# A second feed-forward in two phases: up products partly as seven block products, down products by token

## What is computed

```python
def conv_ffn(h, w_up, conv_w, conv_b, w_down):     # h: 1024 x 1024, w_up: 1024 x 5632, w_down: 2816 x 1024
    u = h @ w_up
    up = jnp.pad(u, ((0, 0), (CONV_W // 2, CONV_W // 2), (0, 0)))
    u = sum(up[:, j:j + T] * conv_w[j] for j in range(CONV_W)) + conv_b      # CONV_W = 3
    gate, val = jnp.split(u, 2, axis=-1)
    return (jax.nn.silu(gate) * val) @ w_down

    f = conv_ffn(modulate(x, mod[3], mod[4]), w_up[l], conv_w[l], conv_b[l], w_down[l])
    x = layer_norm(DEEPNORM_ALPHA * x + mod[5] * f, ln2_g[l], ln2_b[l])
```

## Time and profile before

| | |
|---|---|
| runs (3), median | 3620.06 us (3619.49 to 3621.11) |
| profiled execution, span | 3623.1 us, 3.0 above that median |
| TensorE busy | 3438.2 us, 95% of the span |
| VectorE, ScalarE, GpSimd busy | 47%, 29%, 30% |
| DMA | 186.44 MB, 51 GB/s in the mean |

### The profile page before, as it was taken

How to read it: one execution, slowest core, us unless ns; L and a number is a source line. 1 busy time by engine, 2 the same in 40 slices (tenths; PEclk the granted TensorE clock), 3 DMA queues, 4 the chain that set the end, 5 groups by cost and what they waited for, 6 DMA issues and landing times.

```text
span 3623.1 us, 57600 instructions
## 1 busy us (share of the span) xinstructions
PE 3438.2 (95%) x24727; PEld 2833.2 (78%) x24727; DVE 1690.8 (47%) x2711; ACT 1040.3 (29%) x1485; POOL 1077.2 (30%) x412
## 2 busy tenths in 40 slices
PE   6999999988999999999999899999979989999998
PEld 5777778877778888888887677788867678888887
DVE  4333563066276343343436732463086764434436
ACT  4333564124232111111113323474143321111111
POOL 1221101302343333333333212201313344444443
PEclk9999999989999999999999899999989999999999
DMA  5111001252211111111111111001152111111111
GB/s 192 33 23 30 1 2 59 88 188 59 60 30 41 35 39 38 35 41 36 36 41 70 23 26 39 11 2 30 47 177 79 50 47 47 47 47 51 49 47 64
DMA packets 269680, 186.44 MB, mean 51 GB/s; under 512 B 45404, under 2 KB 249076, under 8 KB 269428
## 3 DMA queue, kind: packets, MB, share of 16 engines
q1 hardware_dynamic: 268272, 182.28, 16.8%
q10 hardware_dynamic: 1156, 0.48, 0.0%
HBM read 174.33 MB, written 8.39 MB: 50 GB/s over the span
## 4 chain that ended last, share of the span: by engine, by line
PE 84%; DVE 9%; issue 3%; ACT 1%; DMA 1%; POOL 1%; SPq 1%; POOLq 0%; DVEq 0%; ACTq 0%
PE psum L1146 61%; PE psum L937 6%; PE psum L1252 5%; PE psum L1410 3%; PE psum L946 2%; PE psum L1338 2%; DVE f_t L2490 1%; PE psum L1174 1%; DMA ada_late<-in_w_ada_dram 1%; DVE y_chan L2376 1%; PE psum L1369 1%; PE psum L1072 1%; DVE c_x L2340 1%; DVE h_lo L2116 1%; PE psum L1494 1%
## 5 line engine op out<-in xcount | busy, mean ns | idle before, releaser
L1146 PE MATMUL psum<-h_hi,w_split 128*128 128x512 f32 (+1 forms) x6016 | 1458.4, 370 | 15.8 <-DVEq L696 6.2
L887 POOL TENSOR_SCALAR w_split<-w_raw 128x1024 fp32r<-128x1024 f32 x196 | 550.3, 2808 | 2371.2 <-PE psum L1146 1640.8
L1146 PEld LDWEIGHTS psum<-h_hi,w_split 128*128 128x128 f32 x6016 | 1038.3, 188 | 229.4 <-issue 20.6
L1146 PE MATMUL psum<-h_lo,w_split 128*128 128x512 f32 (+1 forms) x3008 | 806.8, 368 | 0.0
L1146 PEld LDWEIGHTS psum<-h_lo,w_split 128*128 128x128 f32 x3008 | 520.0, 188 | 98.0
L2490 DVE SCALAR_TENSOR_TENSOR f_t<-psum,vec,f_t 128x1023 f32<-128x1023 f32 (+1 forms) x264 | 260.1, 1013 | 664.9 <-ACT f_t L3086 661.8
L889 POOL TENSOR_TENSOR w_split<-w_raw,w_split 128x1024 fp32r<-128x1024 f32 x196 | 480.5, 2451 | 16.4
L1146 PE MATMUL psum<-f_hi,w_split 128*128 128x512 f32 (+1 forms) x1696 | 416.9, 371 | 13.5 <-DVE f_t L2490 9.2
L3086 ACT ACTIVATE f_t<-psum,vec 128x1280 f32<-128x1280 f32 (+1 forms) x88 | 115.5, 1312 | 905.2 <-PE psum L1146 886.7
L1146 PEld LDWEIGHTS psum<-f_hi,w_split 128*128 128x128 f32 x1696 | 296.7, 188 | 77.4 <-issue 22.0
L2376 DVE SCALAR_TENSOR_TENSOR y_chan<-psum,mods,y_chan 128x1024 f32<-128x1024 f32 (+1 forms) x256 | 247.0, 1001 | 162.3 <-PE psum L1146 162.1
(11 more groups left out here) (300 smaller groups left out, 3564.9 us busy)
## 6 DMA issues: line engine op xcount, KB each, us to landing
w_raw<-in_w_up_dram SPq DMA_DIRECT2D x88, 512.0 KB, 3.8
ada_late<-in_w_ada_dram SPq DMA_DIRECT2D x32, 1024.0 KB, 7.4
w_raw<-in_w_down_dram SPq DMA_DIRECT2D x44, 512.0 KB, 3.8
w_raw<-in_w_in_dram SPq DMA_DIRECT2D x42, 512.0 KB, 3.8
ada<-in_w_ada_dram SPq DMA_DIRECT2D x4, 2048.0 KB, 16.8
ada_early<-in_w_ada_dram SPq DMA_DIRECT2D x8, 1024.0 KB, 5.3
x_first<-in_x_dram SPq DMA_DIRECT2D x8, 512.0 KB, 7.8
o_x<-in_x_dram SPq DMA_DIRECT2D x8, 512.0 KB, 3.9
```

The source lines that it names most:

```text
L887: pool.tensor_scalar(w_hi[:, n % 2], w_raw[:, n % 2], 1.0, None, ALU.mult).then_inc(s["w_hi_done"], 1)
L1146: last = pe.matmul(columns(key, t0, t0 + tn), weight, a[:, k, t0:t0 + tn], start=(k == order[0] and j == 0), stop=(closes and k == order[- ...
```

## The change

Only the last layer's feed-forward changes. Its first six f go as before (but convs, silus and gates follow in another order, and nothing is split for the down product). The other 16 f (`fast_f` = 6 onwards) take both halves of one f, 256 weight columns, by 1024 channels by 1024 tokens, as a 2 x 2 block product: weight blocks a11, a12 (gate half, lower and upper channels), a21, a22 (value half), tokens in two halves of 512. Seven block products of 4 k x 3 passes = 12 matmuls (`product`) take the place of eight. GpSimd forms four sums of weight blocks and all low parts (`fast_weights`), ScalarE the high parts (`high_operand`, called `ahead`), in a ring of four operands. The token operands of the sums are made once, by VectorE and ScalarE, during f = 3 to 5 (`differences`, four blocks; `last_differences` overwrites h itself). A bank is copied out while it is still being accumulated (`take`), and VectorE adds the pieces into `up_u` in SBUF (`joined`), from which `begin` and `conv` now read.

Every gated f is stored in DRAM (`f_mid`), and so is `y_chan`. After the last up product the down products run for all 22 f by token, in two groups of four token tiles that fill the eight PSUM banks: one step n per f and group (24 matmuls, 44 steps), the down weights loaded twice, gated by VectorE, split by ScalarE and GpSimd; the token operands come from `f_mid` and are split by ScalarE and VectorE. Four norms run between the groups, the other four at the end.

Of the diff, what the steps below speak of:

```diff
+FAST_FROM = {DEPTH - 1: 6}
+HALF = LAT // 2
+N_W2, N_F2 = 5, 5
+LAST_STEPS = 2
...
+                load_f(0)
+                load_f(1)
+                load_down(1)
+                load_f(2)
+                load_down(2)
+                sp.wait_ge(s["r_stored"], 2 * 16 * KT)
+                for m in range(KT):
+                    sp.dma_start(y_back[:, m, 0:LAT], r_mid[m]).then_inc(s["y_back"], 16)
+                for n in (3, 4):
+                    load_f(n)
+                    load_down(n)
...
+            def fast_weights():
+
+                one, two = up_sums[:, 0], up_sums[:, 1]
+                for i in range(N_FAST):
+                    raw = up_raw[(i + 1) % 2]
+                    a11, a12, a21, a22 = [raw[:, n // 2, HALF * (n % 2):HALF * (n % 2) + HALF] for n in range(4)]
+
+                    def low(j, whole):
+                        n = 7 * i + j
+                        pool.wait_ge(s["op_hi"], n + 1)
+                        pool.tensor_tensor(up_ops[n % 4][:, 1], whole, up_ops[n % 4][:, 0].bitcast(F32), ALU.subtract)\
+                            .then_inc(s["op_ready"], 1)
+
+                    pool.wait_ge(s[f"raw_landed{(i + 1) % 2}"], AGAIN + 32 * (i // 2 + 1))
+                    if i:
+                        pool.wait_ge(s["op_ready"], 7 * i)
+                    pool.tensor_tensor(one, a21, a22, ALU.add).then_inc(s["sum_done"], 1)
+                    low(0, a11)
+                    pool.wait_ge(s["sum_done"], 4 * i + 1)
+                    pool.tensor_tensor(two, one, a11, ALU.subtract).then_inc(s["sum_done"], 1)
+                    low(1, one)
+                    pool.wait_ge(s["sum_done"], 4 * i + 2)
+                    pool.wait_ge(s["op_ready"], 7 * i + 2)
+                    pool.tensor_tensor(one, a11, a21, ALU.subtract).then_inc(s["sum_done"], 1)
+                    low(2, two)
+                    pool.wait_ge(s["op_ready"], 7 * i + 3)
+                    pool.tensor_tensor(two, a12, two, ALU.subtract).then_inc(s["sum_done"], 1)
+                    low(3, a12)
+                    pool.wait_ge(s["sum_done"], 4 * i + 4)
+                    low(4, one)
+                    low(5, two)
+                    low(6, a22)
...
+            def fast_up(l):
+
+                def product(i, j, bank, x_hi, x_lo, begins=True):
+                    n = 7 * i + j
+                    hi, lo = up_ops[n % 4][:, 0], up_ops[n % 4][:, 1]
+                    wait((s["op_ready"], n + 1))
+                    for k in range(KT // 2):
+                        for pass_, (w, a) in enumerate(((hi, x_hi), (hi, x_lo), (lo, x_hi))):
+                            last = pe.matmul(psum[:, bank, :], w[:, P * k:P * k + P], a[:, k],
+                                             start=begins and k == 0 and pass_ == 0,
+                                             stop=k == KT // 2 - 1 and pass_ == 2, skip_group_check=not begins)
+                    last.then_inc(s["prod_done"], 1)
...
+                for i in range(N_FAST):
+                    if i >= 2:
+                        wait((s["snap_done"], 4 * (i - 2) + 4))
+                    product(i, 0, x_bank(i), *tokens(low, 0))
+                    if i:
+                        wait((s["u_done"], 3 * (i - 1) + 3))
+                    else:
+                        wait(freed("F", l, fast_f - 1, 0))
+                        wait((s["t_ready"], 16))
+                    product(i, 1, Z_BANK, *tokens(low, 1))
+                    wait((s["snap_done"], 4 * i + 1))
+                    product(i, 2, x_bank(i), t2_hi, t2_lo, begins=False)
+                    wait((s["u_done"], 3 * (i - 1) + 1) if i else None)
+                    product(i, 3, Y_BANK, *tokens(high, 0))
+                    wait((s["snap_done"], 4 * i + 3))
+                    product(i, 4, x_bank(i), t3_hi, t3_lo, begins=False)
+                    product(i, 5, Z_BANK, *tokens(high, 1), begins=False)
+                    wait((s["u_done"], 3 * i + 2))
+                    product(i, 6, x_bank(i), t4_hi, t4_lo, begins=False)
...
+                for group in range(2):
+                    for k in range(FT - LAST_STEPS):
+                        n = FT * group + k
+                        wait((s["w2_ready"], n + 1))
+                        wait((s["f2_ready"], n + 1))
+                        for i in range(4):
+                            if k == 0 and group:
+                                wait((s["y_freed"], i + 1))
+                            elif k == 0:
+                                free_banks(i)
+                            last = part(n, i, k == 0, False)
+                        last.then_inc(s["k_done"], 1)
+                        if k == 4:
+                            old_sums(group)
...
+                    also(dve.tensor_tensor(t_scratch[:], lo[:, down, then], lo[:, down, first], ALU.subtract))
+                    tt(one, hi[:, down, then], hi[:, down, first], ALU.subtract)
+                    tt(one, one, t_scratch[:], ALU.add)
+                    also(dve.tensor_tensor(t_scratch[:], lo[:, up, then], lo[:, down, then], ALU.subtract))
+                    tt(three, hi[:, up, then], hi[:, down, then], ALU.subtract)
+                    tt(three, three, t_scratch[:], ALU.add, whole=True)
+                    tt(two, hi[:, up, then], one, ALU.subtract)
+                    tt(two, two, lo[:, up, then], ALU.add, whole=True)
+                    dve.wait_ge(s["t_whole"], 3 * k + 2)
+                    tt(four, hi[:, up, first], two, ALU.subtract)
+                    tt(four, four, lo[:, up, first], ALU.add, whole=True)
+                    for n, (whole, t_hi, t_lo) in enumerate(((three, t3_hi, t3_lo), (two, t2_hi, t2_lo), (four, t4_hi, t4_lo))):
+                        dve.wait_ge(s["t_split_hi"], 3 * k + n + 1)
+                        dve.wait_ge(s["t_whole"], 3 * k + n + 1)
+                        say("t_ready", dve.tensor_tensor(t_lo[:, k], whole, t_hi[:, k].bitcast(F32), ALU.subtract))
...
+                    if n == 0:
+                        dve.wait_ge(s["prod_done"], 7 * i + 4)
+                        ins = dve.tensor_tensor(up_u[:, 0, 0:HALF], psum[:, Y_BANK, :], taken[:, 0], ALU.add)
...
+                    dve.wait_ge(s["r_stored"], 2 * 16 * KT)
+                    differences(0)
+                    conv(4, 0)
+                    differences(1)
+                    conv(4, 1)
+                    gated(4)
+                    differences(2)
+                    conv(5, 0)
+                    differences(3)
+                    last_differences()
+                    conv(5, 1)
+                    gated(5)
...
+                def take(i, n):
+
+                    act.wait_ge(s["prod_done"], 7 * i + (1, 2, 3, 7)[n])
+                    if n == 3:
+                        if i:
+                            act.wait_ge(s["tapped"], 2 * i)
+                        say("snap_done", copy(up_u[:, 1, 0:HALF], psum[:, x_bank(i), :]))
+                        return
+                    if i:
+                        act.wait_ge(s["u_done"], 3 * (i - 1) + (1, 2, 3)[n])
+                    else:
+                        act.wait_ge(s["t_ready"], 12)
+                    say("snap_done", copy(taken[:, n], psum[:, Z_BANK if n == 1 else x_bank(i), :]))
...
+                        ahead(0)
+                        if i:
+                            take(i - 1, 3)
+                            begin(f - 1, 1)
+                        take(i, 0)
+                        ahead(1)
+                        take(i, 1)
+                        ahead(2)
+                        take(i, 2)
+                        ahead(3)
+                        ahead(4)
+                        ahead(5)
+                        if i == N_FAST - 1:
+                            high_weights(0)
+                        begin(f, 0)
+                        ahead(6)
+                        silu(f)
+                    act.preload_act_table_set(LN_EXP_SET)
+                    high_tokens(0)
```

481 lines of the change are left out of this document (390 added, 91 removed).

## The result

The changed kernel takes **3633.55 us** (median of 4 runs, 3631.82 to 3636.14) where the kernel before took 3619.77 beside it: ratio 1.0041, 95% interval 1.0027 to 1.0056, so 0.4% slower, about 14 us. A second set of runs gave 1.0040 (1.0028 to 1.0052). The forecast was 3625 in a range from 3603 to 3650 (3613 to 3638 for its own case), and it put 0.41 on slower, 0.32 on no change and 0.27 on faster.

What follows compares the result with a forecast made beforehand. The prediction took TensorE, busy for 95% of the span, with its matmuls plus 20.6 us of waits, as the bound. New waits of 67.9 us against 62.8 gained gave +5.1 us, so 3625 us, range 3603 to 3650.

Steps and rivals of the forecast that it cites:

- What the change takes away: Whole change: 43.5 us of matmuls and 20.6 us of waits go, the tail gets longer; net gain 62.8 us.
- (c): Steady block products: ScalarE's queue, GpSimd's hold on conv and restarts cost 1.8 us an f, 15 times, 27 us.
- nothing holds conv: Rival on the steady block products: conv steps on SBUF as quick as on PSUM, time 3607 us; chance 0.18.
- the port becomes the bound: Rival on the steady block products: exclusive shared-port work makes products wait for operands, time 3649 us; chance 0.15.
- (a): f = 2 to 5: VectorE's convs free PSUM slots late by 2.1 + 0.9 + 4.3 + 2.7, 10 us.
- (b): Entry into block products: TensorE idles 11 us before product 0, then 2.5 us for half clock; 14 us.
- (d): Start of the down phase: first step waits 5.9 us for the tokens' halves, plus 2.5 for the clock; 8.4 us.
- (e): y_chan read back ahead of the loads for down step 3: covered by the late down start and three steps; nothing.
- (f): Between the token groups: norms free banks late, waits of 0.75, 2.7 and 4.55 us, 0.5 for clock; 8.5 us.
- preparation is cheaper: Rival on f = 2 to 5 and the entry: VectorE's preparation costs 12 us, not 24; time 3613; chance 0.11.
- slow reload: Rival on reading y_chan back: reload goes at the pace of single loads, time 3644 us; chance 0.08.
- TENSOR_SCALAR holds VectorE too: Rival on f = 2 to 5: GpSimd's weight splits hold VectorE for their whole 2.8 us, time 3635; chance 0.06.

Runs made afterwards that it cites:

- e5: Changed kernel, but GpSimd's low half of operand 2 waits until the gate conv of the f before is done: 3618.12 us, 1.0001 of the kernel before.
- e1: Changed kernel, but ScalarE copies product 0 out ahead of the silu and value-half begin of the f before: 3608.48 us, 0.9975 of the kernel before.
- e6: Changed kernel, but at the entry ScalarE copies the high halves of last_differences ahead of operands 1 and 2: 3627.89 us, 1.0026 of the kernel before.
- e3: Changed kernel, but SyncE issues the first output store ahead of the loads for down step 25: 3626.95 us, 1.0028 of the kernel before.
- e2: Changed kernel with block products from f = 8 (14 f, not 16), operand differences spread over f = 4 to 7: 3623.41 us, 1.0013 of the kernel before.
- e4: Changed kernel, token halves for down steps 0 and 1 and step 1's weights prepared before the last convs: 3633.81 us, 1.0047 of the kernel before.
- e8: Changed kernel with e1, e3, e4, e6, last copy before last silu, reload spread and used later, four norms in a row: 3602.30 us, 0.9952.
- e9: e8 with 14 f as block products, difference blocks after conv (4, 0), (5, 0), (6, 0) and gated(6): 3591.82 us, 0.9924 of the kernel before.
- e10: e9 with low halves of tokens 0 and 1 before up_u's last sum, step 2's weight gating and high half before the last value conv: 3585.04 us.
- e11: e10 with the tokens of down step 2 also split ahead of the last value conv: 3587.60 us, 0.9911 of the kernel before.

## Why the prediction was right, and where it was off

The sign, the mechanism of most terms and the place of nearly every wait were as forecast; the sum was 9.9 us too low in the own part, where +5.1 became +15.0. That the sign came out was not secured: +5.1 is the difference of 67.9 and 62.8, and single terms were off by up to 4.4. The forecast itself gave slower only 0.41.

- **What the change takes away**, 62.8 us: 1344 matmuls of L1838 at 226.7 ns, no other work. The tail is the 11.8 us forecast; the kernel before has 10.3 in place of the 10.5 taken, which makes 0.2.
- **(c) The steady block products**: the step is right, 20.78 us an f for 20.9. e5 and e1 show both its parts, the queue (0.5) and the hold (0.9, taken as 1.2). A restart cost 0.3 where 0.1 was taken, so that two errors nearly cancel. Its rivals fall: "nothing holds conv" by the 1739 ns in after against 1284 in e5, "the port becomes the bound" by e1, where an f takes 19.05 under the same load. The working said that 19.8 us of exclusive work was more than the 19.05; that figure was too high.
- **(a)**: "late by 2.1 + 0.9 + 4.3 + 2.7", 10; measured 11.9. The profiled waits were 2.01, 3.77 and 1.76 with 3.4 us of half clock behind the first two; in e1, with the clock full behind the first wait, they were 2.01, 0.91, 4.25 and 1.91, close to the layout. What was too low is the end of the last conv: TensorE got the slot for f = 5's second gemm 90.4 us after the first gemm of f = 2, where the layout has 88.9.
- **(b)**: 11 us of idling before product 0 was right (11.18). The step that failed is "product 1 waits for last_differences, near 3016, hidden by that slow product 0". Product 0 hid only part: product 1 started 121.0 us after f = 2's first gemm, not near 115, after another 3.20 us of waiting, and with 1.5 us of half clock behind it. By the forecast's own sign ("I would be wrong if TensorE waits for an operand inside a set") it was wrong here, once. e6 shows the cause to be ScalarE's order, in which a copy that waits for GpSimd stood ahead. GpSimd's hold on the four steps (5.74 us for 2.8) is seen in the trace; what it alone costs no run shows.
- **(d)** 8.7 for 8.4, right. **(e)** no wait: no step waited for a transfer or for what hangs on one. Whether the reload would show without delay (d) stays open: in every kernel with an earlier start either the fourth tile, step 2 or step 3 waited for something else, or the reload had been moved.
- **(f)**: waits of 7.7 us for the 8.0 forecast, but two (4.76 and 2.97) and not three, and for another reason in part: I let VectorE's own order set all of it, and 2.3 us were a store behind a load in SyncE's queue (e3). The clock and restarts of these waits took 4.8, where I had 0.5.

So the 9.6 us by which waits and clock came out higher are 4.4 in (b), 4.0 in (f), 1.9 in (a) and 0.3 in (d), less 1.0 in (c). The terms that were mis-sized are **last_differences** (2.9 us of waiting that product 0 didn't hide) and **the clock behind the last wait of a series**: 1.5 in (b), 2.5 in (d) and 2.7 in (f), where the forecast counts a drop behind product 0's wait and in (d), and next to none in (f).

Of the other rivals, "preparation is cheaper" fell (512-column steps take 0.69, as taken) and "slow reload" fell. "TENSOR_SCALAR holds VectorE too" had 3635, the number nearest to the measured 3633.55, but not by its mechanism: it asked for 20 us in (a), which has 11.9. As a hold for the whole 2.8 us it fell in this timeline, where a weight split (a TENSOR_SCALAR) runs beside three VectorE steps with two SBUF inputs. Something of it is there, though: one of the three took 0.7 longer, and the split took 3.32 us where it takes 2.77 at 2909 and 2941.

```profile
2961.29 0.69 DVE L2810 TENSOR_TENSOR taken<-taken,h_lo 128x512 f32<-128x512 f32 x1
2961.29 3.32 POOL L1027 TENSOR_SCALAR w_split<-w_raw 128x1024 fp32r<-128x1024 f32 x1 [14.37 <-DMA w_raw<-in_w_up_dram]
2962.01 1.41 DVE L2810 TENSOR_TENSOR taken<-h_hi,taken 128x512 f32<-128x512 f32 x1
2963.45 0.69 DVE L2810 TENSOR_TENSOR taken<-taken,h_lo 128x512 f32<-128x512 f32 x1
```

## What to carry over

Saving TensorE's products is worth what the handshakes around them leave: here 43.5 us of matmuls and 20.6 of old waits went, and 77.5 came back, of which one move in one queue's order (e1) took 24.6 away again without touching any arithmetic. For every copy that frees a bank, ask what stands ahead of it in its engine's order and what that waits for; here the order was costly in the steady state, at the start of the down phase and in the store queue. And price a wait with the clock behind it: in the changed kernel each wait of 2.97 us and more, up to 11.18, had 1.2 to 2.7 us of lost clock behind it, and one of 1.42 us, fifteen times over, had none. But ask first whether another wait follows that would swallow the loss.

## What the runs showed of the hardware

- Waits of 1.42 us before product 2 left the granted clock at 1.00 in every period. In the two to three microseconds after waits of 3.77, 5.97 and 11.18 it was 0.57, 0.50 and 0.50. At 2.0 us both were seen, behind the same wait at f = 4 (2.00 to 2.02 us in all twelve profiles that have it): six had a drop that cost 1.7 us (the changed kernel, e2, e4, e6, e8, e9), six had none (its second profile, e1, e3, e5, e10, e11).
- GpSimd's TENSOR_TENSOR and a VectorE step with two SBUF inputs kept each other out: a conv step took 1739 ns in the mean with GpSimd between, 1284 without (e5). The Trainium skill (SBUF — State Buffer, Who interferes with whom) states this, and the rows agree; its rule taken for GpSimd's TENSOR_SCALAR they don't bear out in full: in the last fence the two ran at the same time, with 0.7 us lost on one side and 0.5 on the other.
- A hold costs only where something awaited stands behind it: in e1 conv's steps were held for longer (1889 ns in the mean), GpSimd's operations and their holds filled 97% of the time, and TensorE lost nothing.
- The time from the program's start to the first gemm of f = 2 differed by up to 14 us between executions of the same matmuls (2886.6 to 2900.7), and that of the part behind it by 0.5 to 0.6. For a change of a few microseconds the own part is the finer measure.
